# Recurrent layer of a hybrid decoder: one buffer per level mask, a diagonal scratch of its own, another order of GpSimd's steps, and the output norm ahead of the SiLU of v

## What is computed

```python
qkv = silu(causal_depthwise_conv(qkv, conv_w))      # width 4
q = l2norm(q) * 128 ** -0.5;  k = l2norm(k)
beta = sigmoid(b_raw);  g = -exp(a_log) * softplus(a_raw + dt_bias)
# per head and chunk, g summed within the chunk:
a_mat = where(strict, (k * beta) @ k.T * decay, 0)
t_inv = inverse(a_mat + eye)                        # triangular solve
u = t_inv @ (v * beta);  w = t_inv @ (k * beta * exp(g))
# from chunk to chunk:
v_new = u - w @ state
out = (q * exp(g)) @ state + (q @ k.T * decay) @ v_new
state = state * exp(g_last) + k_dec.T @ v_new
o = rmsnorm(o, o_gain) * silu(z)
```

## Time and profile before

| what | value |
|---|---|
| median of 3 runs | 2264.69 us (2264.46 to 2264.79) |
| the profiled execution, its own time | 2266.0 us |
| its span | 2264.1 us |
| PE busy | 2165.4 us (96% of the span) |
| DVE, ACT, POOL busy | 1047.9, 821.4, 275.8 us |
| mean granted clock of PE | 0.979 |
| recurrent layer's units in the span | about 1432 to 1841 us |
| chain that ended last | PE 86%, POOL 4%, DVE 3%, ACT 2%, issue 2%, DMA 2%, SP 1% |

### The profile page before, as it was taken

The page is one execution under the profiler, slowest core; times in us unless marked ns, Lnnn a source line. Parts: engine busy times, 40 slices in busy tenths (PEclk is TensorE's granted clock), DMA queues, the critical chain, the costliest instruction groups (busy, mean ns, idle before and its releaser), DMA issues.

```text
span 2264.1 us, 25983 instructions
## 1 busy us (share of the span) xinstructions
PE 2165.4 (96%) x9662; PEld 1724.5 (76%) x9662; DVE 1047.9 (46%) x1573; ACT 821.4 (36%) x1168; POOL 275.8 (12%) x379
## 2 busy tenths in 40 slices
PE   7999999999999999999999999877878899999998
PEld 6888887666667888887888888666767787888886
DVE  4444444687644444432444433444545554444423
ACT  4333223224544333322333322545566453333221
POOL 1000000122210000000000000143344301000001
PEclk9999999999999999999999999988888999999999
DMA  4333322222122323322232332211111122323321
GB/s 168 93 99 96 112 94 68 73 59 63 47 65 89 97 93 101 112 90 78 93 102 93 109 100 80 72 47 43 55 51 48 57 76 92 102 93 97 117 90 50
DMA packets 55966, 190.18 MB, mean 84 GB/s; under 512 B 11728, under 2 KB 11728, under 8 KB 55888
## 3 DMA queue, kind: packets, MB, share of 16 engines
q1 hardware_dynamic: 53680, 189.00, 26.3%
q10 hardware_dynamic: 2208, 0.13, 0.1%
HBM read 186.74 MB, written 2.36 MB: 84 GB/s over the span
## 4 chain that ended last, share of the span: by engine, by line
PE 86%; POOL 4%; DVE 3%; ACT 2%; issue 2%; DMA 2%; SPq 1%; DVEq 0%; POOLq 0%; ACTq 0%
PE prod L433 26%; PE prod L435 25%; PE prod L434 25%; PE misc L635 2%; POOL rows L1503 1%; POOL rows_tmp L1500 1%; DMA blk<-blocks 1%; PE misc L566 1%; PE prod L523 1%; PE misc L584 1%; DVE w_lo L1050 1%; POOL b_lvl L1446 1%; ACT w_hi L776 1%; PE misc L546 0%; PE misc L575 0%
## 5 line engine op out<-in xcount | busy, mean ns | idle before, releaser
L433 PE MATMUL prod<-h_hi,w_hi 128*128 128x512 f32 x1856 | 762.1, 411 | 0.6 <-DVE w_lo L1050 0.3
L1050 DVE TENSOR_TENSOR w_lo<-raw,w_hi 128x1024 fp32r<-128x1024 f32 (+1 forms) x300 | 399.5, 1332 | 768.1 <-ACT w_hi L776 767.5
L435 PE MATMUL prod<-h_hi,w_lo 128*128 128x512 f32 x1856 | 729.9, 393 | 0.0
L434 PE MATMUL prod<-h_lo,w_hi 128*128 128x512 f32 x1856 | 728.9, 393 | 0.0
L776 ACT ACTIVATE w_hi<-raw 128x1024 fp32r<-128x1024 f32 (+1 forms) x317 | 356.5, 1125 | 606.6 <-PE prod L435 595.0
L433 PEld LDWEIGHTS prod<-h_hi,w_hi 128*128 128x128 f32 x1856 | 352.7, 190 | 99.3 <-issue 32.7
L435 PEld LDWEIGHTS prod<-h_hi,w_lo 128*128 128x128 f32 x1856 | 351.5, 189 | 75.7
L434 PEld LDWEIGHTS prod<-h_lo,w_hi 128*128 128x128 f32 x1856 | 352.6, 190 | 67.3 <-issue 4.8
L433 PE MATMUL prod<-a_hi,w_hi 128*128 128x512 f32 x704 | 278.1, 395 | 0.0
L435 PE MATMUL prod<-a_hi,w_lo 128*128 128x512 f32 x704 | 278.1, 395 | 0.0
L434 PE MATMUL prod<-a_lo,w_hi 128*128 128x512 f32 x704 | 278.1, 395 | 0.0
(11 more groups left out here) (228 smaller groups left out, 1896.5 us busy)
## 6 DMA issues: line engine op xcount, KB each, us to landing
raw<-in_w SPq DMA_DIRECT2D x253, 512.0 KB, 3.5
raw<-in_wd SPq DMA_DIRECT2D x64, 704.0 KB, 4.0
blk<-blocks SPq DMA_DIRECT2D x32, 128.0 KB
x<-in_x SPq DMA_DIRECT2D x8, 256.0 KB, 5.3
out<-y_out SPq DMA_DIRECT2D x8, 256.0 KB, 2.2
consts<-in_consts SPq DMA_DIRECT2D x1, 768.0 KB, 8.0
blocks<-a_mat SPq DMA_DIRECT2D x40, 4.0 KB, 1.4
raw<-in_w SPq DMA_DIRECT2D x2, 256.0 KB, 4.1
```

The source lines that it names most:

```text
L433: pe.matmul(bank, wh, hi, start=first and k == 0, stop=False)
L434: pe.matmul(bank, wh, lo, start=False, stop=False)
L435: ins = pe.matmul(bank, wl, hi, start=False, stop=last and k == tiles_n - 1)
L1050: dve.tensor_tensor(w_lo[:, n % 2, 0:w], raw[:, n % 4, 0:w], w_hi[:, n % 2, 0:w].bitcast(F32), ALU.subtract).then_inc(lo_ready, 1)
```

## The change

Mask 7 gets a buffer of its own (the half of silu_g that the layer leaves free), so that each level has one. The diagonal scratch of kk moves from a_mat to act_f. The waits that protected a_mat move from kk to amat. POOL's steps are parted and reordered: masks 5, 6, 7 each with a wait for its own y of the head before, at places 19, 23 and 14 (before: 6 and 5 at 18, 7 at 18 after y5), rows' start value behind mask 6. On PE and ACT gram moves from place 7 to 9, out from 2 to 1, osquare from 3 to 2, osum from 6 to 5, and the SiLU of v from 5 to 7. In one slot the older head's steps come first. The explicit table load ahead of rk stays for the last head only. ACT's three transfers stay at place 18, under the name blocks.

```diff
-CHAIN1 = {"spread": -30, "decay": -27, "mask": -26, "kk": -13, "amat": -11, "lvl": -10, "qdec": -6, "rows": -1,
-          "rk": -1, "cv": 1, "gram": 3, "turn": 11, "y5": 13, "lvl7": 14, "t5": 15, "y6": 17, "t6": 19, "y7": 21, "t7": 23}
+CHAIN1 = {"spread": -30, "decay": -27, "mask": -26, "kk": -13, "amat": -11, "blocks": -10, "lvl5": -9, "qdec": -6,
+          "lvl6": -5, "rows": -1, "rk": -1, "cv": 1, "gram": 5, "lvl7": 10, "turn": 11, "y5": 13, "t5": 15, "y6": 17,
+          "t6": 19, "y7": 21, "t7": 23}
...
-          "out": 22, "osquare": 23, "osum": 26, "fin": 28}
+          "out": 21, "osquare": 22, "osum": 25, "fin": 28}
...
-SILU_SLOT = 5
+SILU_SLOT = {"k": 5, "q": 5, "v": 7}
...
-        b_lvl = od("b_lvl", [2, TT, P])
+        b_low, b_top = od("b_lvl", [2, TT, P]), silu_g[:, 1, :].rearrange("p (t c) -> p t c", t=TT)
+        b_lvl = {5: b_low[:, 0], 6: b_low[:, 1], 7: b_top}
+        diag = act_f[:, 0, :].rearrange("p (t c) -> p t c", t=TT)
...
-                    pe.wait_ge(b_made, UP * g + max(l, 2))
+                    pe.wait_ge(b_made, UP * g + l)
...
                 elif name == "rk":
-                    act.preload_act_table_set(LN_EXP)
+                    if g == HEADS - 1:
+                        act.preload_act_table_set(LN_EXP)
...
                     if g:
                         dve.wait_ge(rk_ready, g)
-                        dve.wait_ge(b_made, UP * g)
-                        dve.wait_ge(blk_out, 16 * BLOCKS * g)
                     for t in range(TT):
-                        ins = dve.tensor_tensor_reduce(a_mat[:, t, :], M[0][:, t, :], const["ident"], 1.0, EPS,
+                        ins = dve.tensor_tensor_reduce(diag[:, t, :], M[0][:, t, :], const["ident"], 1.0, EPS,
...
                 elif name == "amat":
                     dve.wait_ge(dec_exp, g + 1)
+                    if g:
+                        dve.wait_ge(b_made, UP * g)
+                        dve.wait_ge(blk_out, 16 * BLOCKS * g)
...
-                elif name == "lvl":
+                elif name in ("lvl5", "lvl6", "lvl7"):
+                    l = int(name[3:])
                     pool.wait_ge(a_made, g + 1)
                     if g:
-                        pool.wait_ge(y_mm, UP * g)
-                    for l in (LOW + 2, LOW + 1):
-                        mask(l)
-                    pool.tensor_copy(rows[:], const["block_eye"][:, 0:BLK].unsqueeze(1).broadcast_to([P, TT, BLK]))\
-                        .then_inc(rows_seq, 1)
+                        pool.wait_ge(y_mm, UP * (g - 1) + l - LOW)
+                    mask(l)
+                    if l == LEVELS - 1:
+                        pool.tensor_copy(rows[:], const["block_eye"][:, 0:BLK].unsqueeze(1).broadcast_to([P, TT, BLK]))\
+                            .then_inc(rows_seq, 1)
...
-                elif name == "lvl7":
-                    pool.wait_ge(y_mm, UP * g + 1)
-                    mask(LEVELS)
```

More of the change, by code:

```diff
@@ L685, in stage_pe @@
                         pe.wait_ge(vb_ready, g + 1)
-                    each(M[3], b_lvl[:, l % 2], u_inv[:, i]).then_inc(y_mm, 1)
+                    each(M[3], b_lvl[l + LOW], u_inv[:, i]).then_inc(y_mm, 1)
                     if l > 1:
@@ L965, in stage_act @@
                     act.activation(dec_a[:], dec_a[:], ACT.Exp, scale=-1.0).then_inc(dec_exp, 1)
-                elif name == "lvl":
+                elif name == "blocks":
                     act.wait_ge(a_made, g + 1)
@@ L1023, in _ @@
                         act.activation(dst, pre, ACT.Copy, scale=od_conv[:, conv_channel(kind, h), 3:4]).then_inc(tap_done, 1)
-                    if k == SILU_SLOT and kind in "qkv":
+                    if kind in "qkv" and k == SILU_SLOT[kind]:
                         act.wait_ge(conv_done, u - 1)
@@ L1445, in mask @@
             def mask(l):
-                pool.tensor_tensor(b_lvl[:, (l - LOW) % 2], a_mat[:], same(const[f"level{l}"]), ALU.mult).then_inc(b_made, 1)
+                pool.tensor_tensor(b_lvl[l], a_mat[:], same(const[f"level{l}"]), ALU.mult).then_inc(b_made, 1)
             def add_squares(r):
```

## The result

The changed kernel takes 2235.59 us (median of 4 runs, 2234.34 to 2235.95) where the kernel before took 2264.74 (2264.46 to 2267.94): a ratio of 0.9867, 95% interval 0.985 to 0.9884, or 29 us less. The forecast was 2239.5 us, 25.2 less, in a range of 2227 to 2256. PE is busy for 2149.9 us and its mean granted clock is 0.987 (before 0.979).

The account below looks back on a forecast made before the run. It took the POOL and ACT chain, as long as PE's way, to bound the first half, and PE, stopping for resid, the second. 31.4 + 3.4 - 9.6 = 25.2 us saved gives 2239.5 us, range 2227 to 2256.

Parts of the forecast that it names:

- The stop for resid and the slow stretch behind it: Second half, turn to y7: PE's stop of 2.76 us and 1.6 of slow clock go, 26.2 us over six heads.
- The wait moved to amat is empty: Second half: mask 7 is made 1.3 us after turn, amat reached about 3.7 after, so amat does not wait.
- SiLU of v and gram two places later: Before turn: k's taps and SiLU come earlier, so kk's wait of 0.55 us goes in three heads, 1.65 us.
- POOL's order is nearly cancelled by out and osquare: First half: e_row wins 1.3 us, the squares lose 1.04; 0.26 in five heads, 2.1 in head 1, 3.4 summed.
- Fewer table loads give nothing: ACT, under the rows chain: four of six loads per head go, 1.28 us each, hidden by slack, gain nothing.
- The new stop at turn: At turn: PE waits 2.5 to 4 us for t_inv; slow clock behind costs 1.6 in six heads, 9.6 us.
- My top price: Behind turn: the upper bound of the clock loss, 3.1 us, from 6.2 us at 0.56 after a stop of 4.08.
- Collisions: DVE and POOL: mask 5 against w_lo costs 0 to 1.21 us per head, 0 to 7 in all; taken as 0.
- rival 3: After amat: mask 5 and w_lo exclude each other, y6 waits 1.2 us in six heads; 7 us, 2246.7; chance 0.10.
- rival 4: In rows: POOL shut out by w_lo and taps, t_inv 6.6 us later per head; 2279 us, slower; chance 0.04.
- Rival 1: At turn: the stop is near 4 us and costs 3.1 each time, 9 us more; 2248.5 us; chance 0.20.
- rival 2: Behind turn: no clock loss; gain 34.8 us, time 2229.9; chance 0.16.

Follow-up runs that it names:

- third_buffer: The kernel before with only mask 7's own buffer new, scratch in a_mat and both waits at kk as before: 2235.64 us, 0.9868.
- pool_order: The changed kernel with all steps of PE and ACT at their old places and rk's table load in each head: 2223.70 us, 0.9815.
- squares_behind: The changed kernel with out and osquare back at places 2 and 3: 2222.98 us, 0.9808.
- three_loads: The changed kernel with three explicit table loads ahead of rk in every head, instead of one in the last head only: 2238.01 us, 0.9875.
- out_back: The changed kernel with out alone back at place 2, osquare still ahead of the exponentials: 2237.68 us, 0.988.

## Why the prediction was right, step by step

*The stop for resid and the slow stretch behind it.* Right in place and size: L707 waits 0.5 us at most, and a half without a slow stretch is 14.0 us where I had 14.4. The cause I named had one part too many: I gave the gain to own buffers and moved waits together, and third_buffer shows that mask 7's buffer does it all.

*The wait moved to amat is empty.* Right: mask 7 is made at 1644.29 behind t_inv, amat starts behind it, 3.9 us after turn at full clock where I had 3.7, and 4.3 to 5.0 where the clock is down.

*SiLU of v and gram two places later.* The 1.65 us came, for PE's waits for k's SiLU (L1030, before L1026) fell from 4.8 to 3.2 us, but nothing shows that this edit brought them: pool_order, with both at their old places, has 3.2 too.

*POOL's order is nearly cancelled by out and osquare.* Right: e_row at 4.17 (forecast 4.06), dec_a's end at 9.57 (9.5), turn at 25.07 (24.96). The five full first halves gave 2.3 us where I had 1.3, because two of those before were 25.8 long. squares_behind and pool_order then showed that this cancellation is a choice: undone, it is worth 12 us.

*Fewer table loads give nothing.* ScalarE has 25 fewer (forecast 24). Borne out by three_loads, which puts three per head back, within 2.4 us, and by pool_order, which has all of them and is 12 us faster. L978 begins 1.30 us after a load began, and e_row 1.30 behind the start of its own. Both follow a real change of set, while the load of the earlier trace rows that I argued from reloads a set that was active. That disagrees with the drain which the Trainium skill ("ScalarE: Activation LUTs", "What ACT_TABLE_LOAD costs") adds to the load at every switch to a different set.

*The new stop at turn.* Forecast 2.5 to 4 us, measured 2.3 to 3.9 from head 1 on. Its bill was the term that I mis-sized: 1.6 us in six heads, 9.6. Measured are 1.5 in four heads and nothing in two, 6.0, and 2.0 behind the last turn, where I had put nothing. The 2.0 are for the most part clock as well: 0.63 over 4.6 us, 1.7. My top price was also too high: 6.2 us at 0.56 lose 2.7 us and not 3.1. That term, and halves that were 0.4 us shorter than my 14.4, are most of what was gained over the forecast between the first turn and the last (31.5 against 25.2). A first turn 1.0 us earlier and the 2.0 behind the last one bring the spans to 30.5 apart; these misses partly cancel, which is luck, and the medians are 29 apart.

*Collisions.* Mask 5 took 2.13 us and not 1.27, with a w_lo of 1.22 that had begun 0.22 before it; the trace agrees with the exclusive lock of the Trainium skill ("SBUF — State Buffer", "SBUF: two separate sides"). DVE's next tap took 1.56 us, and y6 did not wait, so 0 was the right end and rival 3 did not occur. rows kept its length: 1630.24 to 1643.08 is 12.8 us, as before, and rival 4 has nothing for it.

*Rivals.* Rival 1 (3.1 us behind each turn) did not occur here, but out_back shows it at up to 2.8 us, in three heads of six; rival 2 (no loss) did in two heads of six. They are one mechanism with an outcome that varies.

## What to carry to other kernels

When two engines work in a ring, find each half's own bound first: a stop in the half that another chain covers is free, and taking it away only moves it to where that chain ends. Before an edit takes a wait away from one instruction, ask what is late; one more buffer that lets it be made early did here as much as the whole change. Put work that the ring does not wait for yet (here a mask for the next head, and the squares) behind the step that it waits for.

## What the runs showed that I had not expected

A stop's bill at the clock is not a function of its length. Stops of 3.5 to 3.9 us ahead of turn were followed by a loss of 1.5 us in the changed kernel's halves and of 0, 1.5 and up to 2.8 in out_back's; three stops of 2.3 us by none, none and 1.5; in the kernel before, one of 3.6 us by none and one of 2.76 by 1.6. It also varies from run to run: out_back's four times span 7 us. So a version that shortens a chain by 0.8 us per head can be no faster, if a long stop stays. What decides it within this range was not settled.
